# Transposes within 16-token blocks on VectorE, identities added at eviction, and solve products in diagonal quarters, in a chunked RWKV-7 recurrence

## The reference

```python
def step(S, inp):
    r_t, d_t, k_t, v_t, a_t, b_t = inp
    sa = jnp.einsum('bhij,bhj->bhi', S, a_t)
    S = (S * d_t[:, :, None, :] + sa[..., None] * b_t[:, :, None, :]
         + v_t[..., None] * k_t[:, :, None, :])
    return S, jnp.einsum('bhij,bhj->bhi', S, r_t)
```

## Time and profile before

| | us |
|---|---|
| median of three runs | 1442.86 (1439.71 to 1444.89) |
| the profiled execution | 1440.23 |
| its span in the profile | 1438.5 |
| from the first stage of the recurrence to `u20` | 107.6 to 211.2 |
| from there to the second token tile of the output projection | 211.2 to 233.2 |

### The profile page before, as it was taken

How to read it: one execution, slowest core, us unless ns; L and a number is a source line. 1 busy time by engine, 2 the same in 40 slices (tenths; PEclk the granted TensorE clock), 3 DMA queues, 4 the chain that set the end, 5 groups by cost and what they waited for, 6 DMA issues and landing times.

```text
span 1438.5 us, 27772 instructions
## 1 busy us (share of the span) xinstructions
PE 1347.0 (94%) x11287; PEld 1213.2 (84%) x11287; DVE 926.5 (64%) x1345; ACT 755.8 (53%) x1183; POOL 49.0 (3%) x91
## 2 busy tenths in 40 slices
PE   7998778999998998999989999999998998999998
PEld 6777666999996887999978997899996877799997
DVE  7985556677777566776684757655555757555555
ACT  6754235555557646555574644544444654444443
POOL 7000000100000000000000000100001000000000
PEclk9999999999999999999999999999999999899999
DMA  9500017555553406556546545565654550356650
GB/s 273 196 5 4 19 47 261 194 193 187 175 196 127 146 31 234 176 182 197 180 145 195 184 147 175 159 195 175 201 180 146 176 178 29 117 176 186 193 175 30
DMA packets 135219, 222.40 MB, mean 155 GB/s; under 512 B 6186, under 2 KB 105746, under 8 KB 134865
## 3 DMA queue, kind: packets, MB, share of 16 engines
q1 hardware_dynamic: 132832, 214.32, 46.4%
q0 software_dynamic: 2144, 6.61, 1.4%
q10 hardware_dynamic: 144, 0.06, 0.0%
HBM read 219.90 MB, written 1.05 MB: 154 GB/s over the span
## 4 chain that ended last, share of the span: by engine, by line
PE 86%; DVE 7%; ACT 3%; issue 3%; DMA 1%; ACTq 0%; DVEq 0%; SPq 0%
PE ps L504 83%; PE ps L819 1%; DVE ulo L490 1%; DVE x_sb L1953 1%; DVE xn_lo L1941 1%; DMA raw<-in_w_o_rwkv 1%; DVE scratch L2362 0%; ACT uhi L482 0%; DVE xs L1929 0%; PE ps L1225 0%; DMA scratch<-in_mu 0%; ACT scratch L1453 0%; DVE x_sb L1959 0%; DVE raw L2206 0%; DVE scratch L1986 0%
## 5 line engine op out<-in xcount | busy, mean ns | idle before, releaser
L490 DVE TENSOR_TENSOR ulo<-raw,uhi 128x1024 fp32r<-128x1024 f32 x398 | 486.2, 1225 | 356.9 <-ACT uhi L482 356.4
L482 ACT ACTIVATE uhi<-raw 128x1024 fp32r<-128x1024 f32 x398 | 420.8, 1059 | 424.5 <-PE ps L504 419.3
L504 PE MATMUL ps<-xn_hi,uhi 128*128 128x256 f32 x1472 | 418.3, 284 | 2.2 <-DVE xn_lo L2002 1.0
L504 PE MATMUL ps<-xn_lo,uhi 128*128 128x256 f32 x1472 | 417.1, 283 | 0.0
L504 PE MATMUL ps<-xn_hi,ulo 128*128 128x256 f32 x1472 | 417.0, 283 | 0.0
L504 PEld LDWEIGHTS ps<-xn_hi,uhi 128*128 128x128 f32 x1472 | 283.2, 192 | 5.8 <-issue 2.2
L504 PEld LDWEIGHTS ps<-xn_lo,uhi 128*128 128x128 f32 x1472 | 283.2, 192 | 1.7
L504 PEld LDWEIGHTS ps<-xn_hi,ulo 128*128 128x128 f32 x1472 | 283.0, 192 | 0.0
L504 PE MATMUL ps<-uhi,xm_hi 128*128 128x512 f32 x512 | 200.5, 392 | 2.9 <-DVE xm_lo L2310 1.1
L504 PE MATMUL ps<-ulo,xm_hi 128*128 128x512 f32 x512 | 199.9, 391 | 0.0
L504 PE MATMUL ps<-uhi,xm_lo 128*128 128x512 f32 x512 | 159.1, 389 | 0.0
(11 more groups left out here) (297 smaller groups left out, 1261.2 us busy)
## 6 DMA issues: line engine op xcount, KB each, us to landing
raw<-in_mlp_w SPq DMA_DIRECT2D x64, 1024.0 KB, 5.4
raw<-in_w_up SPq DMA_DIRECT2D x44, 1024.0 KB, 5.1
raw<-in_w_down SPq DMA_DIRECT2D x22, 1024.0 KB, 4.9
raw<-in_gmlp_w_in SPq DMA_DIRECT2D x16, 1024.0 KB, 5.3
raw<-in_fox_w_in SPq DMA_DIRECT2D x16, 1024.0 KB, 5.2
raw<-in_w_rkv SPq DMA_DIRECT2D x12, 1024.0 KB, 5.7
raw<-in_gmlp_w_out SPq DMA_DIRECT2D x8, 1024.0 KB, 5.1
raw<-in_w_o_rwkv SPq DMA_DIRECT2D x4, 1024.0 KB, 8.1
```

The source lines that it names most:

```text
L482: nc.scalar.activation(ring_unit(uhi, m, n), raw_unit(n, j), ACT.Copy).then_inc(hi_done, 1)
L490: nc.vector.tensor_tensor(ring_unit(ulo, m, n), raw_unit(n, j), ring_unit(uhi, m, n).bitcast(F32), ALU.subtract).then_inc(lo_done, 1)
L504: return nc.tensor.matmul(o, l, r, start=start, stop=stop, skip_group_check=True)
```

## The change

The inverse is still built from the same factors. What changes is how operands come about and where products lie:

- `ad`, `y1`, `ya`, `xz` go. `Ad` is made from `AdT` by a VectorE transpose, which turns each 32x32 block in place (enough, since blocks of 16 tokens hold everything). `A2T`, `A4T` and `Z` are made the same way from `A2`, `A4` and `Xn`. That is four transposes of 128x512 per token tile and group.
- The running product is Y + A^k Y instead of (I + A^k) Y: the product's eviction adds the earlier `Y` (VectorE, 128x512, from PSUM). `lz` and `z2` do likewise. Stages `a4`, `a8`, `x`, `lz`, `z2` are evicted in part or wholly by VectorE, and ScalarE evicts `A2`, `A4`, `A8T`, `L`, `LT`, `L2` in one operation each.
- Per head and chunk there are eleven products: `a2` 1, `a4` 2, `a8` 2, `x` 1, `l` 2, `lz` 2, `z2` 1. All are written to `halves[h]`.
- The stage order is written anew, `a2`, `x` and `z2` take one PSUM bank, `sv` takes none of banks 0 to 3, `gn_sums`, `gn_scale`, `gn_gain`, `gn_bonus` of the first tile move, VectorE no longer splits unit 24 at `st21`, and `gated_transposes(0)` come after `y31` instead of after `u31`.

```diff
-        ad00 ad01 bonus00 a200 a201 sk00 y100 a400 y101 a401 sk01 tok00 ya00 ya01 tok01
-        rv00 xz00 rv01 xz01 l00 yk00 l01 yk01 lz00 lz01 z200 sb10 z201 sb11
-        sv00 u00 sv01 u01 ad10 ad11 st00 st01 a210 sk10 a211 rs10 rs11 y110 a410 sk11 y111 a411
-        sv10 u10 sv11 u11 y00 y01 ys10 ys11 tok10 ya10 tok11 ya11 st10 st11 rv10 xz10 rv11 xz11 y10 y11
+        kn00 kn10 kn20 kn30 sb00 sb01 bonus00 sk00 a200 a201 sk01 a400 a401 tok00 a800 a801 tok01
+        rv00 rv01 x00 x01 yk00 yk01 l00 l01 lz00 lz01 sb10 z200 sb11 z201
+        sv00 u00 sv01 u01 a210 a211 st00 st01 sk10 a410 sk11 a411 rs10 rs11
+        sv10 u10 sv11 u11 y00 y01 ys10 ys11 tok10 a810 tok11 a811 st10 st11 rv10 x10 rv11 x11 y10 y11
         l10 yk10 l11 yk11 rs20 lz10 rs21 lz11 z210 ys20 z211 ys21
...
+        CORE_MM = {"a2": (("AdT", "Ad"),), "a4": (("A2T", "A2"), ("A2T", "Y0")), "a8": (("A4", "A4T"), ("A4T", "Y1")),
+                   "x": (("A8T", "Y2"),), "l": (("Xn", "AoT"), ("AoT", "Xn")), "lz": (("L", "LT"), ("LT", "Z")),
+                   "z2": (("L2", "Z1"),)}
...
+                    for n, (l, r) in enumerate(CORE_MM[name]):
+                        for e in range(8):
+                            for h in range(2):
+                                last = mm(o[n][halves[h], HD * e:HD * e + HD], core_buf(g, l)[halves[h], e, :],
+                                          core_buf(g, r)[halves[h], e, :], True, True)
...
-                if st == ("u", 3, 1):
-                    pe.wait_ge(y_done, 1)
-                    for b in range(2):
-                        gated_transposes(0, b)
+            pe.wait_ge(y_done, 1)
+            for b in range(2):
+                gated_transposes(0, b)
...
+            core_act = {"a2": ("A2",), "a4": ("A4",), "a8": ("A8T",), "l": ("L", "LT"), "lz": ("L2",)}
...
+                if name in ("a4", "a8", "x", "lz", "z2"):
+                    q = len(o) - 1
+                    dst, a = {"a4": ("Y1", "Y0"), "a8": ("Y2", "Y1"), "x": ("Xn", "Y2"), "lz": ("Z1", "Z"),
+                              "z2": ("TT", "Z1")}[name]
...
+                        ins = TT(core_buf(g, dst), by_head(o[q]), core_buf(g, a), ALU.add)
+                    ins.then_inc(moved[ring_bank[k][q]], 1)
+                if name in ("a2", "a4", "x"):
                     dve.wait_ge(moved[ring_bank[k][0]], ring_use[k][0])
...
+                    dst, a = {"a2": ("A2T", "A2"), "a4": ("A4T", "A4"), "x": ("Z", "Xn")}[name]
+                    nc.vector.transpose(core_flat(g, dst), core_flat(g, a)).then_inc(ti_done, 1)
...
                         for u in range(2):
                             last = TT(half_heads(core_buf(g, "AdT"), u), v[u][:, :, 1, :], heads8(2), ALU.mult)
-                        last.then_inc(adt_done, 1)
+                        step(last)
+                        nc.vector.transpose(core_flat(g, "Ad"), core_flat(g, "AdT")).then_inc(adt_done, 1)
...
+                    if name == "sb":
+                        dve.wait_ge(adt_done, 2 * (2 * i + g) + 1)
+                        TT(core_buf(g, "Y0"), core_buf(g, "Ad"), eye(8), ALU.add).then_inc(adt_done, 1)
```

More of the change, by code:

```diff
@@ L236, in core_buf, with core_flat @@
             return by_head(r[:, c + 512 * CORE_SLOT[name]:c + 512 * CORE_SLOT[name] + 512])
-        def core_two(g, names, u):
+        def core_flat(g, name):
             r, c = core_at(g)
[L241 to L246, removed]
+            return r[:, c + 512 * CORE_SLOT[name]:c + 512 * CORE_SLOT[name] + 512]
         def core_keys():
@@ L292, in build @@
                 free = range(2, 8)
-            free = [b for b in free if b not in held]
+            free = [b for b in free if b not in held and (b >= 4 or st[0] != "sv")]
             ring_bank[k] = sorted(free, key=lambda b: ring_last[b])[0:CORE_BANKS.get(st[0], 2)]
@@ L2125, in gn_sums, with gn_scale @@
                 nc.vector.tensor_reduce(stat[:, 16:32], h16(S(S_MA, 1024)), AXX, ALU.add).then_inc(yvar_done, 1)
-            def gn_scale(n):
-                dve.wait_ge(ystd_done, n + 1)
-                step(nc.vector.reciprocal(stat[:, 16:32], stat[:, 32:48]))
+            def gn_scale(n, u):
                 a = acc(n).rearrange("p (u j i) -> p u j i", u=2, i=HD)
                 root = stat[:, 16:32].rearrange("p (u j) -> p u j", u=2).unsqueeze(3).to_broadcast([P, 2, 8, HD])
-                TT(by_pair(YG[:, n, :])[:, :, 0, :], a[:, 0], root[:, 0], ALU.mult)
-                for q in range(2):
-                    ho, hi = slice(64 * q, 64 * q + 64), slice(64 - 64 * q, 128 - 64 * q)
-                    last = TT(by_pair(YG[:, n, :])[ho, :, 1, :], a[hi, 1], root[hi, 1], ALU.mult)
-                step(last)
+                if u == 0:
+                    dve.wait_ge(ystd_done, n + 1)
+                    step(nc.vector.reciprocal(stat[:, 16:32], stat[:, 32:48]))
+                    TT(by_pair(YG[:, n, :])[:, :, 0, :], a[:, 0], root[:, 0], ALU.mult)
+                else:
+                    for q in range(2):
+                        ho, hi = slice(64 * q, 64 * q + 64), slice(64 - 64 * q, 128 - 64 * q)
+                        last = TT(by_pair(YG[:, n, :])[ho, :, 1, :], a[hi, 1], root[hi, 1], ALU.mult)
+                    step(last)
             def gn_gain(n):
@@ L2161, in beside @@
                     bonus_add(g)
-                elif name == "ya" and i == 1:
+                elif name == "a8" and i == 1:
                     bonus_gate(g)
@@ L2196, in _ @@
-                if name in ("a2", "a4", "l"):
-                    for b, use in zip(ring_bank[k], ring_use[k]):
-                        dve.wait_ge(moved[b], use)
-                    dst, a = {"a2": ("A2I", "A2T"), "a4": ("A4I", "A4T"), "l": ("LTI", "LT")}[name]
-                    TT(core_buf(g, dst), core_buf(g, a), eye(8), ALU.add).then_inc(ti_done, 1)
-                    continue
-                dve.wait_ge(core_ps, k + 1)
-                if name in ("ya", "lz"):
-                    names = {"ya": ("A8I", "Y"), "lz": ("L2I", "Z1")}[name]
-                    for u in range(2):
-                        TT(core_two(g, names, u), two(ring_bank[k][u]),
-                           tm[:, 4:6, :].unsqueeze(2).to_broadcast([P, 2, 4, HD]), ALU.add)\
-                            .then_inc(moved[ring_bank[k][u]], 1)
+                dve.wait_ge(core_ps, k + 1)
```

100 lines of the change are left out of this document (35 added, 65 removed).

## The result

| | before | after |
|---|---|---|
| median of the runs, in turns on one chip, nine each | 1443.99 us | 1449.09 us |
| ratio of the times | | 1.0035 (1.0021 to 1.0050) |
| the profiled execution | 1440.23 | 1447.46 |

The kernel became slower by 0.35%, 5.1 us. I had forecast no change that can be measured. 1449.09 lies inside my range, near its upper end, and on the side to which I gave 0.19.

A forecast was written before the change was run, and what follows sets the result against it. Bounds in the recurrence: TensorE's program loading (about 3.8 us per 256 instructions) and VectorE's in-order queue. Terms -1.3 + 5.3 - 4.9 - 1.1 + 1.5 = -0.5 us gave 1439.7 profiled, forecast median 1442.4, range 1437 to 1450.

The forecast's parts named there:

- Start: Up to the end of `bonus00`: removing `ad00` and `ad01` only leaves TensorE idle during ScalarE's V copy; gain 0.
- B: From the end of `lz01` to the end of `u01`: 12.3 us forecast, `u01` ending 4.0 us behind.
- Stretch A: From 118.4 us to the end of `lz01`: 1.5 blocks fewer, less waits for VectorE transposes; gain 1.3 us.
- The tail: From `u20` to the projection's second token tile: `gn_square(1)` starts later, behind the copies of the transposes; cost 1.5 us.
- The count of instructions: TensorE in the recurrence: 1152 instructions fewer, 4.5 blocks, at 3.8 us a block 17 us less fetching.
- The wait at `u01`: TensorE stops about 5 us ahead of `u01` until VectorE evicts `z201`, queued behind `sb11` and `bonus_times`.
- C: From the end of `u01` to `rv10`: fewer blocks, plus waits and a half-clock stretch; 29.5 us against 34.4.
- C2: From `rv10` to the end of `u20`: 352 products become 320, 20.9 us become 19.8.
- stops still every 256: Sign in the recurrence: TensorE would still stop every 256 instructions in the profile after.
- Instruction count decides: Rival, faster: blocks run at 3.60 us and new waits fall into fetch time; -6.7 us, 1436; chance 0.17.
- Diagonal blocks run slower than the pace: Rival, slower: all 19 blocks from 118 us on at 4.2 instead of 3.8 us; +7.6, 1450; chance 0.13.
- The stops are no fetching: Rival, slower: fewer instructions gain nothing, and TensorE pays 7 us more for its products; 1455; chance 0.04.

The follow-up runs named there:

- warm_start: Changed kernel with nine spare matmuls in front of `bonus00`, ahead of all its waits; 1.0019 to the kernel before.
- ad_late: Kernel before with stages `ad00` and `ad01` put behind `bonus00` instead of ahead of it; 1.0027 to the kernel before.
- four_quarters: Changed kernel with products of `a4`, `a8`, `l`, `lz` written to all four quarters, same instructions, wrong output; 1.0029 to the kernel before.
- z201_first: Changed kernel with `z201` issued and evicted ahead of `sb11` and `bonus_times`; 1.0004 to the kernel before.
- transposes_back: Changed kernel with `gated_transposes(0)` put back behind `u31`; 1.0007 to the kernel before.
- abc: Changed kernel with `a200`, `a201` ahead of `bonus00`, `z201` ahead of `sb11`, and `gated_transposes(0)` behind `u31`; 0.9979 to the kernel before.
- keep_warm: Changed kernel with spare matmuls, 10 ahead of `bonus00` and 22 ahead of `u01`'s wait for `z201`; 1.0033 to the kernel before.

## Why the prediction was wrong

**The step that failed: "Start", with its "gain 0".** I had the idle time right (TensorE waits for ScalarE's copy of V) and its length, and I called it free because `bonus00` starts when it did. It isn't free. The clock falls to 0.50 just behind the start of `bonus00`, which takes 6.4 in place of 3.7 us, and that puts it 2.8 to 3.0 us later. I had priced exactly such a stretch behind the stop in B from the earlier trace rows, and didn't ask whether the idle time that I had found myself in front of `bonus00` would do the same. The runs show it both ways (`warm_start`, `ad_late`). Of these 3 us, filling the gap gave back 2.3 to 2.4 in the medians of two runs.

**Stretch A** is 0.5 to 0.9 over my number. The clock can be a part of that at most: 4.3 to 4.5 us of it run at 1.2 GHz where it was 3.4 in the kernel before. No run separates the rest.

**The tail was mis-sized**: 1.5 us forecast, 1.6 and 3.2 measured. The mechanism stood as I wrote it, `gn_square(1)` behind the copies of the transposes. The first pair of profiles has half-clock stretches in the tail, 6.8 us after and 3.4 before, the second has none; I put the 1.6 us between the pairs down to that, which no run tests.

**What held.** The count of instructions. The transpose at 0.70 where I took 0.69. The estimate of 1.24 us from the Trainium skill's figure for one of 128x128 (VectorE: DVE Perf Modes, The three transpose paths) was 0.5 too high. The wait at `u01`, its cause and its size: 12.6 for B against 12.3. In C the three waits, 0.9, 1.9 and 4.2 where I had 1.1, 2.2 and 4.3, and the slow clock, 3.8 us of work at 1.2 GHz, so 1.9 for my 1.7. What is left of C, 19.4 us for my 20.2, is a pace of 3.66 us a block and not 3.8.

**What held by luck.** C2. Half a block fewer is 1.9 us at my own pace, and I took 1.1 without a reason. It took 20.8 and 20.7 us, where the kernel before took 20.9 and 19.6: little or nothing was won. TensorE is busy 20.1 of the 20.8 us, against 17.7 of 20.9 before, so here the products fill the time, and the half-clock stretch is 6.8 us in place of 3.4. `four_quarters` took 19.4 us there, with a half-clock stretch of 3.4, so the two aren't told apart. The shorter C hides it in the sum. The sign "stops still every 256" isn't to be seen either: apart from the waits at `u01` and `rv10`, no stop without a releaser is longer than 0.8 us between `bonus00` and `u20` (1.1 in the second profile). 128 diagonal passes take 3.95 us themselves. One count was wrong without touching the sum: the kernel before has 448 products in C, not 480 (905 passes in the trace, with 8 transposes); only with 448 do the stretches add up to the 1152 instructions.

**The rivals.** *Instruction count decides*: no, the waits added to the pace. *Diagonal blocks run slower than the pace*: its size was reached, its reason is wrong; a block of 128 diagonal passes took 3.95 us, not 4.2, and `four_quarters` shows what the diagonal costs, about 1 us in the median. *The stops are no fetching*: no, they returned 256 instructions apart when the products became faster.

**Sum.** The second token tile came at 238.3 and 236.5 us, where I had it at 232.7: 5.6 and 3.8 us late, of which the start has 3.0 and 2.8, A 0.9 and 0.5, B 0.3 each, C and C2 together -0.2 and -0.1, and the tail 1.7 and 0.3. The medians show 5.6 over my -0.5. What stays open: how long a half-clock stretch gets. In the six profiles with an idle TensorE straight ahead of `bonus00` (both of after, `z201_first`, `transposes_back`, `four_quarters`, `ad_late`), the first one lasted 10.2 us four times and 6.8 twice, began inside `bonus00`, and `bonus00` ended at 119.9 to 121.9. In the seven with TensorE busy there it lasted 3.4 us five times and 6.8 twice, and `bonus00` ended at 118.3 to 120.5. In six of these seven it began at 118.3 to 119.0, but in `abc` at 116.6, and `bonus00` took 5.54 us with no idle time ahead of it. The mean shift is clear, a single execution isn't.

## What to carry to other kernels

Removing work that fills a wait isn't always free, even if nothing starts later: look at what runs at the far end of the gap and price it at 1.2 GHz too, or put other ready work there, as `a200` and `a201` here. When a step is handed to an engine with an in-order queue, list what now stands ahead of each eviction that TensorE waits for; moving eight side operations, three stages and the transposes of the first tile by a few places was worth 18 us here (1.0036 to 0.9908). And where something other than the products sets the pace (here stops every 256 instructions, which I take for the loading of the program, and waits for VectorE), making products faster or slower moves little, so look for the stops first.

## What the runs showed of the hardware

- TensorE fell to 1.2 GHz (granted clock 0.50) for 6.8 or 10.2 us where it had stood idle for 2.1 us (2.4 from start to start) and a stage of 32 matmuls with 2 columns followed at once, in six of six profiles. With ten 128x512 matmuls between the idle time and that stage it didn't (`keep_warm`), and neither did it behind a stop of 2.02 us ahead of 64x64 products. With TensorE busy ahead of that stage it fell too, in six of seven profiles only near the stage's end, and in five for 3.4 us.
- The same code got half-clock stretches of different lengths in different executions, and the program behind the recurrence took 1203.3 to 1211.9 us with the same instructions. The Trainium skill (TensorE: Matmul & The Clock Gate, Part 1: The HAM clock gate) says of the start of a kernel that the number of slow matmuls varies from run to run; here stretches in the middle do.
- A VectorE transpose of 32x32 blocks over 128x512 fp32 took 0.70 us, about as long as the other operations over as many elements, and its neighbour with an operand in PSUM 0.68.
- With 64x64 fp32 products a block of 256 TensorE instructions took 3.6 to 3.8 us even where its passes ran for 2.5 to 2.7; making products of the changed kernel faster by 12.9 us in all bought 1 us in the median.
